# Late adaLN columns summed on GpSimd, gates spread by a product with ones, in a hybrid decoder layer

## What is computed

```python
mod = silu(c) @ w_ada + b_ada                       # (1, 1024) @ (1024, 6144)
sh_m, sc_m, gt_m, sh_f, sc_f, gt_f = split(mod, 6)
h = rmsnorm(x, norm_pre_mix) * (1 + sc_m) + sh_m
proj = h @ w_in
y = concat(hgrn2(...), sparse_attention(...)) @ w_out
x = x + gt_m * rmsnorm(y, norm_post_mix)
h = rmsnorm(x, norm_pre_ffn) * (1 + sc_f) + sh_f
gate, up = split(h @ w_ffn_in)
x = x + gt_f * rmsnorm((silu(gate) * up) @ w_ffn_out, norm_post_ffn)
```

## Time and profile before

| Engine | busy, us | share of the span | instructions |
|---|---|---|---|
| TensorE (products) | 758.8 | 94% | 3554 |
| VectorE | 408.1 | 51% | 782 |
| ScalarE | 283.4 | 35% | 463 |
| GpSimd | 11.4 | 1% | 39 |

### The profile page before, as it was taken

How to read it: one execution, slowest core, us unless ns; L and a number is a source line. 1 busy time by engine, 2 the same in 40 slices (tenths; PEclk the granted TensorE clock), 3 DMA queues, 4 the chain that set the end, 5 groups by cost and what they waited for, 6 DMA issues and landing times.

```text
span 803.3 us, 10163 instructions
## 1 busy us (share of the span) xinstructions
PE 758.8 (94%) x3554; PEld 584.6 (73%) x3554; DVE 408.1 (51%) x782; ACT 283.4 (35%) x463; POOL 11.4 (1%) x39
## 2 busy tenths in 40 slices
PE   4889999999999889998997999999999999999995
PEld 3555477777866576665885888888888888888884
DVE  3857669797988525427347332222333225344344
ACT  6345452534233233244257233322233333112123
POOL 5000000000000000000000000000000000000000
PEclk9899999999999989997998999999999999999998
DMA  9935015243343150552410432233333233423202
GB/s 310 347 88 150 1 45 167 73 136 102 106 134 107 28 179 19 165 204 84 160 50 27 131 100 84 80 102 104 104 104 91 77 94 123 139 80 103 78 1 105
DMA packets 103845, 88.02 MB, mean 110 GB/s; under 512 B 2980, under 2 KB 93192, under 8 KB 103816
## 3 DMA queue, kind: packets, MB, share of 16 engines
q1 hardware_dynamic: 103816, 87.65, 35.6%
HBM read 85.55 MB, written 2.10 MB: 109 GB/s over the span
## 4 chain that ended last, share of the span: by engine, by line
PE 84%; DVE 9%; issue 2%; DMA 2%; ACT 1%; SPq 1%; DVEq 0%; ACTq 0%
PE ps L1240 45%; PE ps L1261 21%; PE ps L1346 3%; PE ps L1453 2%; PE ps L1291 2%; PE ps L1521 1%; PE ps L1431 1%; DMA w_raw<-in_w_in 1%; DVE w_lo L779 1%; PE ps L1496 1%; PE ps L1580 1%; PE ps L1516 1%; PE ps L1588 1%; DVE score L1002 1%; DVE top L997 1%
## 5 line engine op out<-in xcount | busy, mean ns | idle before, releaser
L1240 PE MATMUL ps<-h_hi,w_hi 128*128 128x512 f32 x576 | 235.2, 408 | 1.1 <-DVE h_lo L832 1.1
L1240 PE MATMUL ps<-h_hi,w_lo 128*128 128x512 f32 x576 | 225.1, 391 | 0.0
L1240 PE MATMUL ps<-h_lo,w_hi 128*128 128x512 f32 x576 | 225.0, 391 | 0.0
L779 DVE TENSOR_TENSOR w_lo<-w_raw,w_hi 128x1024 fp32r<-128x1024 f32 (+1 forms) x110 | 128.7, 1187 | 168.8 <-ACT w_hi L434 168.6
L434 ACT ACTIVATE w_hi<-w_raw 128x1024 fp32r<-128x1024 f32 (+1 forms) x110 | 110.5, 1026 | 97.4 <-PE ps L1261 91.7
L1240 PEld LDWEIGHTS ps<-h_hi,w_hi 128*128 128x128 f32 x576 | 108.5, 188 | 43.5 <-issue 21.7
L1240 PEld LDWEIGHTS ps<-h_hi,w_lo 128*128 128x128 f32 x576 | 108.4, 188 | 23.6
L1240 PEld LDWEIGHTS ps<-h_lo,w_hi 128*128 128x128 f32 x576 | 108.7, 189 | 20.5 <-issue 1.0
L1261 PE MATMUL ps<-w_hi,h_hi 128*128 128x512 f32 x240 | 94.8, 395 | 0.8 <-DVE mix L1138 0.8
L1261 PE MATMUL ps<-w_lo,h_hi 128*128 128x512 f32 x240 | 94.0, 392 | 0.0
L1261 PE MATMUL ps<-w_hi,h_lo 128*128 128x512 f32 x240 | 93.9, 391 | 0.0
(11 more groups left out here) (223 smaller groups left out, 696.6 us busy)
## 6 DMA issues: line engine op xcount, KB each, us to landing
w_raw<-in_w_ffn_in SPq DMA_DIRECT2D x44, 512.0 KB, 4.0
w_raw<-in_w_in SPq DMA_DIRECT2D x28, 512.0 KB, 6.4
w_raw<-in_w_ffn_out SPq DMA_DIRECT2D x22, 512.0 KB, 3.6
adaw<-in_w_ada SPq DMA_DIRECT2D x20, 512.0 KB, 5.0
act<-in_w_ada SPq DMA_DIRECT2D x12, 512.0 KB, 9.0
res<-in_x SPq DMA_DIRECT2D x8, 512.0 KB, 4.8
adaw<-in_w_ada SPq DMA_DIRECT2D x4, 1024.0 KB, 5.3
act<-in_w_ada SPq DMA_DIRECT2D x4, 1024.0 KB, 5.2
```

Source lines behind the costliest of these rows:

```text
L779: V.tensor_tensor(w_lo[slot][:, 0:n], w_raw[slot][:, 0:n], w_hi[slot][:, 0:n].bitcast(f32), ALU.subtract).then_inc(lo_ok, 1)
L1240: last = mm(ps[bank][0:rows, :], a, b, start=(k == 0 and n == 0), stop=(k == KT - 1 and n == 2))
```

## The change

The adaLN columns behind the first 2048 are no longer multiplied on TensorE. They come in four groups of 1024: the mixer's gate, shift and scale of the FFN, the FFN's gate. GpSimd does them one block of 128 rows at a time, 128 partitions by 1024 columns: it multiplies the block in place by silu(c), one number per partition, and adds it to a running total (`add_sum`, 24 times, for the first three groups; `add_tail`, 8 times, for the last). The total of a gate starts at zero with the bias in its partition 0, loaded by a DMA; those of shift and scale start with the first product.

Adding over partitions stays TensorE's. For gates it is a product of a 128x128 matrix of ones with 512 columns of the total (`gate_rows`), which leaves the sum in every partition, that is, spread already; VectorE multiplies it by the second norm's gain, which a DMA has spread into `gate_mix` and `gate_ffn`. For shift and scale sixteen products of one column (`ffn_sums`) give columns. The first gate and `ffn_sums` stand in the last attention head, ahead of its last products; the second gate ahead of the last pass of the gate/up projection. The diagonals, their products and copies, `ada_out`, `ada_half` and `ada_sums` behind the start are gone, and so are two of the seven small parameter loads at the start.

SP's order changes: a load brings two row blocks (1 MB) into one of two slots and waits until the additions on what it replaces are done (`load_sum`); one goes out in the third recurrent head's time, the second behind the last recurrent head's products, the other ten between the loads of attention and output weights. The last eight blocks (512 KB each) follow one gate/up pass each (`load_tail`).

```diff
+            def load_sum(n):
+                col = (2, 3, 4)[n // 4] * D_MODEL
+                if n == 0:
+                    sp.wait_ge(ada_used, START_ADA)
+                elif n == 1:
+                    sp.wait_ge(o_mm, HG_HEADS)
                 else:
-                    sp.wait_ge(ada_used, START_ADA + HG_ADA + 2 * h)
...
+                    sp.wait_ge(sum_used, 2 * n - 2)
+                sp.dma_start(sum_slot[n % 2].rearrange("p (k n) -> p k n", k=2),
+                             w_ada_k[:, 2 * (n % 4):2 * (n % 4) + 2, col:col + D_MODEL]).then_inc(sum_loaded[n % 2], 16)
...
+            def add_sum(h, n):
...
+                if n == 0 and not first_head:
+                    pool.tensor_scalar(total, w, silu, None, ALU.mult).then_inc(sum_used, 1)
+                else:
+                    pool.tensor_scalar(w, w, silu, None, ALU.mult).then_inc(sum_scaled, 1)
+                    pool.wait_ge(sum_scaled, n + 1 if first_head else h * (KT - 1) + (n + 1))
+                    pool.tensor_tensor(total, w, total, ALU.add).then_inc(sum_used, 1)
...
-            for n in range(4):
-                sc.wait_ge(gate_mm, 4 * n + 4)
-                dst = (gate_mix if n < 2 else gate_ffn)[:, (n % 2) * SEQ:(n % 2 + 1) * SEQ]
-                sc.activation(dst, ps[(2, 3, 4, 6)[n]][:, :], ACT.Copy).then_inc(gate_ok, 1)
...
+                if last:
+                    ve.wait_ge(post_loaded, 32)
+                    for b in range(2):
+                        ve.wait_ge(gate_mm, b + 1)
+                        V.tensor_tensor(gate_mix[:, b * SEQ:(b + 1) * SEQ], ps[2 + b][:, :],
+                                        gate_mix[:, b * SEQ:(b + 1) * SEQ], ALU.mult).then_inc(gate_ok, 1)
+                    ve.wait_ge(ada_sum, 1)
+                    V.tensor_tensor(mod[:, 24:40], ps[6][:, 0:16], prm[:, 24:40], ALU.add).then_inc(mod_ok, 1)
...
-            def ada_sums(bank):
-                for c in range(4):
-                    last = mm(ps[bank][:, c:c + 1], ada_rows[:, c * P:(c + 1) * P], ones[:, 0:1], start=True, stop=True)
+            def gate_rows(total, bank, b):
+                mm(ps[bank + b][:, :], ones[:, :], total[:, b * SEQ:(b + 1) * SEQ], start=True,
+                   stop=True).then_inc(gate_mm, 1)
+
+            def ffn_sums():
+                for n in range(2 * KT):
+                    total = (sum_shift, sum_scale)[n // KT]
+                    last = mm(ps[6][:, n:n + 1], total[:, n % KT * P:(n % KT + 1) * P], ones[:, 0:1], start=True,
+                              stop=True)
                 last.then_inc(ada_sum, 1)
...
-                    if st in (1, 3):
-                        te.wait_ge(ada_loaded, h * 64 + (32 if st == 1 else 64))
-                        if st == 1:
-                            te.wait_ge(mod_ok, h + 1)
-                        ada_half(5, st // 2, adaw)
-                    elif st == 7:
-                        te.wait_ge(rows_ok, h + 1)
-                        ada_sums(5)
...
+                if last:
+                    te.wait_ge(sum_used, SUMS)
+                    te.wait_ge(lg_ok, TT * ATT_HEADS)
+                    gate_rows(sum_gate_mix, 2, 0)
+                    gate_rows(sum_gate_mix, 2, 1)
+                    ffn_sums()
...
+            te.wait_ge(sum_used, SUMS + KT)
+            gate_rows(sum_gate_ffn, 4, 0)
+            gate_rows(sum_gate_ffn, 4, 1)
             fin_pass(FT // 2 - 1, False, True)
```

More of the change, by code:

```diff
@@ L55 @@
 ADA_COLS = 512
[L56 removed]
+START_ADA = KT
+SUM_LOADS, SUMS = 12, 24
 IDX_COLS = IDX_HEADS * IDX_DIM + IK_COLS
@@ L425, in _, with add_tail @@
             pool.sem_inc(masks_ok, 1)
+            pool.wait_ge(sin_ok, 4)
+            pool.memset(sum_gate_mix, 0.0).then_inc(mix_zero, 1)
+            def add_sum(h, n):
+                pool.wait_ge(sum_loaded[n // 2 % 2], h * 32 + 16 * (n // 4 + 1))
+                w = sum_slot[n // 2 % 2][:, n % 2 * D_MODEL:(n % 2 + 1) * D_MODEL]
+                silu = silu_pad[:, n * 32:n * 32 + 1]
+                first_head = h == 0
+                total = sum_gate_mix if first_head else part(act, h * D_MODEL, D_MODEL)
+                if n == 0 and first_head:
+                    pool.wait_ge(mix_bias, 16)
+                else:
+                    pool.wait_ge(sum_used, h * KT + n)
+                if n == 0 and not first_head:
+                    pool.tensor_scalar(total, w, silu, None, ALU.mult).then_inc(sum_used, 1)
+                else:
+                    pool.tensor_scalar(w, w, silu, None, ALU.mult).then_inc(sum_scaled, 1)
+                    pool.wait_ge(sum_scaled, n + 1 if first_head else h * (KT - 1) + (n + 1))
+                    pool.tensor_tensor(total, w, total, ALU.add).then_inc(sum_used, 1)
+            def add_tail(k):
+                pool.wait_ge(tail_loaded, k * 16 + 16)
+                pool.wait_ge(sum_used, k + SUMS)
+                pool.tensor_scalar(tail_slot, tail_slot, silu_pad[:, k * 32:k * 32 + 1], None, ALU.mult).then_inc(sum_scaled, 1)
+                pool.wait_ge(sum_scaled, k + (SUMS - 1))
+                pool.tensor_tensor(sum_gate_ffn, tail_slot, sum_gate_ffn, ALU.add).then_inc(sum_used, 1)
+            pool.wait_ge(silu_ok, 1)
+            for h in range(3):
+                for n in range(KT):
+                    add_sum(h, n)
+            pool.wait_ge(att_out, ATT_HEADS)
+            pool.memset(sum_gate_ffn, 0.0).then_inc(ffn_zero, 1)
+            pool.wait_ge(ffn_bias, 16)
+            for k in range(KT):
+                add_tail(k)
         @block.scalar
@@ L1119, in att_body @@
                         split_lo(G_OUT + 1 + t, 1 + t)
-                    elif not last and t == 2:
+                    if not last and t == 2:
                         split_lo(h * 3 + (G_ATT + 5), 2)
@@ L1206, in _ @@
             swiglu(FT // 2 - 1, 0)
+            for b in range(2):
+                ve.wait_ge(gate_mm, b + 3)
+                V.tensor_tensor(gate_ffn[:, b * SEQ:(b + 1) * SEQ], ps[4 + b][:, :],
+                                gate_ffn[:, b * SEQ:(b + 1) * SEQ], ALU.mult).then_inc(gate_ok, 1)
             ve.wait_ge(act_ok[0], 2)
@@ L1584, in _ @@
             att_body(0, True, False)
-            te.wait_ge(mod_ok, HG_HEADS + 2)
-            te.wait_ge(diag_ok, 16)
-            for n in range(16):
-                mm(ps[(2, 3, 4, 6)[n // 4]][:, (n % 4) * P:(n % 4 + 1) * P], ones[:, :], diag[:, n * P:(n + 1) * P],
-                   start=True, stop=True).then_inc(gate_mm, 1)
             with te.Fori(1, ATT_HEADS - 1) as h:
```

145 lines of the change are left out of this document (58 added, 87 removed).

## The result

The changed kernel took 824.66 us (median of 4 runs, 823.51 to 825.46), the kernel before 803.25 us beside it (802.88 to 804.00). The ratio is 1.0261, 95% interval [1.0243, 1.0278]: slower by 21 us, above the top of the range that was forecast (809.0).

The account below looks back on a forecast made before the run. TensorE was taken as the bound, VectorE close behind. Edits -3.9 - 8.4 - 10.3 + 3.1 + 2.2 = -17.3 us, GpSimd's hold on VectorE +11.3, sum -6.0: 797.0 us from a median of 803.05; range 784.5 to 809.

Parts of the forecast that it names:

- the edits: Whole kernel: TensorE work removed less what comes back, without the cost of GpSimd's work, -17.3 us.
- 3.9 forecast: Recurrent heads 0 to 2: adaLN halves and sums gone from TensorE, 1.3 us saved each; nothing for head 3.
- 10.3 and 8.4: Attention heads: 10.3 us from the gates' spreading between heads 0 and 1, 8.4 from halves and sums in heads 0 to 2.
- +3.1: Last attention head: two ones products and sixteen one-column sums add 5.4 us, less work removed there; net +3.1 us.
- The rest: Ahead of the last pass of the gate/up projection: two more ones products, +2.2 us.
- Other signs: Recurrent heads at 37.0 instead of 38.3 us; attention head 1's first product right behind head 0's last.
- the price of the pair: GpSimd's multiplication (0.9 to 1.6 us) plus addition (1.6 to 3.2) over 128x1024: 2.5 to 4.8, taken as 3.6.
- Rival (c): Last attention head: GpSimd too slow, TensorE waits for 24 additions; at 5.8 us a pair 17 late, 814 us; chance 0.09.
- (a): VectorE's two-input operations don't wait for GpSimd, so the eleven us are absent: 785.7 us; chance 0.25.
- (b): Attention heads 0 to 3: rotations and first weight split each wait a whole GpSimd operation, +23 us, 808.8; chance 0.20.
- The SP queue: Weight loads queued on SP behind a block's load that waits for GpSimd's additions would be late too; no price.
- The neighbours: Attention heads: GpSimd holds VectorE's two-input rotation operations, 15 times 0.75 us, +11.3; splits and normalisations count at nothing.

Follow-up runs that it names:

- e4_nowork: Changed kernel with GpSimd's products and additions cut to 8 of 1024 columns, waits, loads and TensorE's work kept: 786.75 us.
- e8_mulonly: Changed kernel with GpSimd's additions cut to 8 of 1024 columns, its multiplications whole: 787.30 us.
- e7_addonly: Changed kernel with GpSimd's multiplications cut to 8 of 1024 columns (two left uncut), its additions whole: 800.86 us.
- e3_both: Changed kernel with output projection weights loaded ahead of the last three block loads and the sixteen one-column sums moved into the output projection: 801.95 us.
- e2_late: Changed kernel with the sixteen one-column sums moved from the last attention head into the output projection, SP's order unchanged: 815.64 us.
- e9_onesbeside: Kernel before with gates spread by ones products, all sums on TensorE, plus 44 GpSimd operations nobody waits for: 812.80 us, against 793.80 without them.

## Why the prediction was wrong

**Right: the edits.** Forecast -17.3, measured -16.9 (e4_nowork), and term by term in its trace: 4.5 us up to the first attention head (3.9 forecast; head 3 gave nothing, as said), 21.6 in heads 0 to 2 for 18.7 (10.3 and 8.4), since a head sheds 3.2 where 2.8 was counted and the low clock of head 0 goes too (0.88, now 1.00). The last head cost 6.7 instead of 3.1 (31.66 for 25.01), but 3.4 of that are the fall of the clock at its end; in e8_mulonly and e7_addonly, with the same products, it cost 3.3 and 2.9, so the +3.1 was right. The rest cost 1.5 for 2.2. That the sum of this trace comes so close is in part luck: what heads 0 to 2 gave beyond the forecast, the fall of the clock took. Other signs came as forecast: recurrent head 1 took 37.2 us (144.07 to 181.28), and head 1's first product follows head 0's last at once.

**The step that failed: the price of the pair.** The forecast took 3.6 us, 4.6 with VectorE's holds, between 2.5 and 4.8. Measured: 5.5 free, 5.9 beside a busy VectorE, and 5.65 a block over the run of 18, since two of these have no addition (the forecast counted 22 pairs where there are 20 and two multiplications alone). The addition lies where it was sought (1.6 to 3.2; 2.36). The multiplication doesn't: 0.9 to 1.6 was worked out from a fill of 256 columns and a select of 128, and 2.85 came, above the addition itself. Both bounds were of other operations, scaled up by columns. A fill of 1024 columns takes 0.96 in these runs, so the scaling was sound; the likeness was not. *By the figure of the Trainium skill (GPSIMD Engine Reference, section 3.1) the addition had been estimated at about 2.3 us, and the trace agrees (2.36); its section 4.1 calls one-input operations roughly line-rate, and on a multiplication by a column the measurement says otherwise: 2.85 us, where VectorE's one-input operation over 1024 columns took 0.75 alone.*

**Rival (c) was the case**, with a chance of 0.09, and its 814 lay outside the stated range, which took in the centres of (a) and (b) alone. Its place (the last head's wait for 24 sums) and its threshold (5.0 us a pair, 5.65 measured) fit, and so did the point at which the head would want them, about 368: e4_nowork reaches it at 354.3, and the 13.5 us that the changed kernel is behind it when the last head starts (347.30 against 333.82) make 367.8. Its price was low, 814 for 824.7. The sums end at 388.2, 20.4 after that for the 17 forecast; the products behind the wait then run at the lower clock (L1426 3.78 for 1.72, L1432 6.62 for 4.19), 4.5 us more; and the first two pairs, which the forecast let run at the end of recurrent head 2 for nothing, began in the midst of it (177.13) and held VectorE's steps. Here is one of one input, 0.55 us in the kernel before:

```profile
180.08 2.65 DVE L1047 TENSOR_SCALAR act<-act,hp 128x512 f32<-128x512 f32 x1
```

That and what hangs on it is 3.3 us up to the first attention head. In all, the changed kernel's span less that of e4_nowork: 3.3 + 10.2 (heads 0 to 2) + 24.9 (last head) = 38.4 of 38.3 us (against a last head at the clock of e8_mulonly's the third would be 3.4 more). The SP queue, which the rival names in one sentence without a price, is worth little alone (2.3 us), and 13.7 once the other wait is gone (e2_late to e3_both).

**The neighbours: right in kind, too small, and put down to the wrong operation.** Forecast +11.3, of which 8.3 in heads 0 to 2. These lost 10.2 there (90.4 against 80.2), with 13 of the additions in them; with additions alone, 20 of them in these heads, 18.9. Over the whole kernel it is +15.2 with pace taken away (e3_both). An operation on two SBUF inputs does wait for an addition, so (a) is out. Head 1 came as forecast: its rotations lost 2.7 us where 4 x 0.75 = 3.0 were forecast, and it is 2.7 longer than in e4_nowork at the same granted clock, 1.00. Head 0 lost 4.4 for 2.3. Missing there were a longer wait for the first maxima (L1137, 4.8 us for 2.7), which were counted at nothing, and the lower clock (0.90 for 1.00), said in one sentence of (b) and put at nothing. And the forecast let both of GpSimd's operations hold the two-input ones; only the addition does. (b), the whole wait each time, falls too: the mean of the rotations' first operation is 1.12 us against 0.68.

```profile
L1114 DVE TENSOR_TENSOR act<-res,rope 32x512 f32<-32x512 f32 x8 | 8.9, 1117 | 9.0 <-PE ps L1543 8.8
```

**Open.** Why the multiplication, which also reads SBUF, lets two-input operations pass, was not looked into; only that it mostly does. Nor was it tried to cut the multiplications into pieces, or to put halves beside additions alone. What lowered the clock at the end of e4_nowork's last head is not known, nor whether its other three executions had the same.

## What to carry to other kernels

When work moves to an engine that had none, price the series before anything else: count of operations, times the duration of that very form, against the point where the first consumer needs the last result. If no row has the form, the upper bound is not the nearest row scaled up, and the case beyond the threshold deserves a larger chance and a place in the range. A run with the work taken out is a reference stage by stage, and only where its clock is that of the run it is held against. Two waits that end together hide each other: taken away one at a time they gave 2.3 and 9.0 us, together 22.7. Where an engine waits for its neighbour's instruction to end, the length of the instruction is a knob: halves turned 802 us into 791, while quarters lengthened the neighbour's own series until it was waited for again (806).

## What the runs showed of the hardware

- GpSimd's multiplication of 128x1024 fp32 by a column takes 2.85 us, longer than the addition of two such tiles (2.36), and three times a fill (0.96).
- VectorE's operations on two SBUF inputs, and its one-input tensor_scalar, wait for the end of a GpSimd addition (2.79 us instead of 0.68; 2.65 instead of 0.55). Beside a multiplication the two-input ones stay at 0.68 to 0.89 for the most part (means of 0.73 and 0.84 in e8_mulonly), and one-input ones are stretched (1.18 instead of 0.35 in one). Operations that read PSUM did not wait in any row looked at (0.67 beside both).
- Beside fills the two-input ones keep 0.68 and the one-input ones stretch two- to threefold (a normalisation 1.08 instead of 0.42, the sixteen diagonals 8.49 instead of 3.23).
- Waits of 2 to 3 us (one of 2.7 in that head) were followed by a mean granted clock of 0.90, which cost as much again (2.5 us in head 1 of e9_onesbeside).
- The same products, behind the same idle time, can run at another clock: the last head's end took 8.96 us in e4_nowork and 6.11 in e8_mulonly (4.35 + 4.61, 3.63 + 2.48).
